# GLA mixing: the coarsest level's differences and exponentials made by ScalarE with biases per channel, and VectorE's wait for the masks put at the first masking

## The reference, cut to what matters

```python
def step(S, inp):
    q_c, k_c, v_c, b_c = inp
    o_inter = jnp.einsum('bhcd,bhde->bhce', q_c * jnp.exp(b_c), S)
    diff = b_c[:, :, :, None, :] - b_c[:, :, None, :, :]
    dmat = jnp.exp(jnp.where(mask, diff, -jnp.inf))
    scores = jnp.einsum('bhid,bhjd,bhijd->bhij', q_c, k_c, dmat)
    o_intra = jnp.einsum('bhij,bhje->bhie', scores, v_c)
    b_last = b_c[:, :, -1:, :]
    S = (S * jnp.exp(b_last[:, :, 0, :])[..., None]
         + jnp.einsum('bhcd,bhce->bhde', k_c * jnp.exp(b_last - b_c), v_c))
    return S, o_inter + o_intra
```

## Time and profile before

| | us |
|---|---|
| median of 3 executions | 3025.73 |
| lowest and highest | 3022.07, 3026.02 |
| the profiled execution, its own time | 3016.57 |
| its span in the profile | 3014.5 |
| PE, DVE, ACT, POOL busy over the span | 2873.7, 1460.5, 1157.9, 260.6 |
| the stage `gla_mix`, from the first to the last instruction of its own | about 210 to 328 |

### The profile page before, as it was taken

One profiled execution on the slowest core, in us unless ns is written; L12 is line 12 of the kernel. 1 busy time (PEld: TensorE's weight loads), 2 busy tenths in 40 slices (PEclk: granted clock), 3 DMA queues, 4 the chain that ended last, 5 costly groups with the idle time before them and its releaser, 6 DMA issues.

```text
span 3014.5 us, 57436 instructions
## 1 busy us (share of the span) xinstructions
PE 2873.7 (95%) x25392; PEld 2356.4 (78%) x25392; DVE 1460.5 (48%) x2048; ACT 1157.9 (38%) x1944; POOL 260.6 (9%) x306
## 2 busy tenths in 40 slices
PE   5987899799998999999999999999999999999997
PEld 5776677788885888888888888788888888888886
DVE  3669576455455644332443337674454534244323
ACT  4766664222224433322322245432244323233322
POOL 1000123544530000000000000000000000000000
PEclk8997899899998999999999999999999999999998
DMA  4320344211102232233222232223223232233222
GB/s 137 136 73 3 110 147 154 57 39 39 40 12 78 91 119 91 91 98 98 91 92 98 98 105 91 88 95 93 97 91 97 92 98 96 93 98 124 95 96 84
DMA packets 100439, 273.11 MB, mean 91 GB/s; under 512 B 9120, under 2 KB 36384, under 8 KB 100192
## 3 DMA queue, kind: packets, MB, share of 16 engines
q1 hardware_dynamic: 91408, 236.94, 24.3%
q0 software_dynamic: 8784, 32.51, 3.3%
HBM read 256.69 MB, written 12.58 MB: 89 GB/s over the span
## 4 chain that ended last, share of the span: by engine, by line
PE 66%; DVE 2%; ACT 1%; issue 0%; DVEq 0%; ACTq 0%
PE be_ps L3009 48%; PE be_ps L3062 16%; PE be_ps L3075 1%; DVE be_ring L2788 1%; PE be_ps L2733 1%; PE be_ps L2727 0%; PE be_ps L2412 0%; DVE be_raw_r L3257 0%; ACT be_whi L3112 0%; DVE be_total L2746 0%; DVE big L2760 0%; DVE big L2770 0%; DVE ext_r L2798 0%; DVE big_r L2798 0%; PE be_ps L2451 0%
## 5 line engine op out<-in xcount | busy, mean ns | idle before, releaser
L3257 DVE TENSOR_TENSOR be_raw_r<-be_raw,be_whi 128x1024 fp32r<-128x1024 f32 x361 | 442.4, 1225 | 974.2 <-ACT be_whi L3112 973.9
L3112 ACT CAST be_whi<-be_raw 128x1024 fp32r<-128x1024 f32 x361 | 378.9, 1050 | 891.6 <-DMA be_raw<-in_ffn_down 316.8
L3009 PE MATMUL be_ps<-ext_r,be_whi 128*128 128x512 f32 x2304 | 713.7, 391 | 6.8 <-DVE be_raw_r L3257 3.6
L3009 PE MATMUL be_ps<-big_r,be_whi 128*128 128x512 f32 x2048 | 642.1, 394 | 0.8 <-DVE be_raw_r L3257 0.5
L3009 PEld LDWEIGHTS be_ps<-ext_r,be_whi 128*128 128x128 f32 x2304 | 430.2, 188 | 102.6 <-DVE be_raw_r L3257 4.8
L3009 PEld LDWEIGHTS be_ps<-big_r,be_whi 128*128 128x128 f32 x2048 | 383.1, 188 | 95.7 <-DVE big_r L2796 1.0
L3009 PE MATMUL be_ps<-ext_r,be_raw_r 128*128 128x512 f32 x1152 | 448.4, 389 | 0.0
L3009 PE MATMUL be_ps<-big_r,be_raw_r 128*128 128x512 f32 x1024 | 408.0, 398 | 0.0
L3062 PE MATMUL be_ps<-ext_r,be_whi 128*128 128x512 f32 x1152 | 354.7, 389 | 0.0
L3009 PEld LDWEIGHTS be_ps<-ext_r,be_raw_r 128*128 128x128 f32 x1152 | 216.2, 188 | 45.2
L3062 PEld LDWEIGHTS be_ps<-ext_r,be_whi 128*128 128x128 f32 x1152 | 216.2, 188 | 45.2
(11 more groups left out here) (342 smaller groups left out, 3822.1 us busy)
## 6 DMA issues: line engine op xcount, KB each, us to landing
be_raw<-in_ffn_gate SPq DMA_DIRECT2D x88, 512.0 KB, 3.5
be_raw<-in_ffn_up SPq DMA_DIRECT2D x88, 512.0 KB, 3.5
be_raw<-in_ffn_down SPq DMA_DIRECT2D x88, 512.0 KB, 3.5
be_raw<-in_conv_in SPq DMA_DIRECT2D x48, 512.0 KB, 3.5
gp_ada<-in_ada POOLq DMA_DIRECT2D x24, 512.0 KB, 3.8
rp_ada<-in_ada POOLq DMA_DIRECT2D x24, 512.0 KB, 4.5
rwkv_prepared<-big SPq DMA_DIRECT2D x16, 512.0 KB, 3.2
be_raw<-in_w_out SPq DMA_DIRECT2D x16, 512.0 KB, 3.6
```

The lines of the kernel that those rows point to most:

```text
L3009: mm = pe.matmul(ps[:, bank], part[:, k * P:(k + 1) * P], xs(k), start=(k == order[0] and i == 0), stop=(k == order[-1] and i == 2))
L3112: act.copy(w.hi[:, n % 3], w.raw[:, n % 3]).then_inc(w.hi_ready, 1)
L3257: dve.tensor_tensor(w.lo(n), w.raw[:, n % 3], w.hi[:, n % 3].bitcast(F32), ALU.subtract).then_inc(w.lo_ready, 1)
```

## The change

ScalarE makes level 6 alone: two small copies write the two middle values, with either sign and divided by 16, to a new tile `middle`; after a wait for them, eight exponentials of 64 elements read `summed` directly, with the middle as bias per channel, and write the slot of the ring. VectorE's `diff6` is gone from all 8 turns. `copy_block(j)` waits for `diff5` and `exp6` of turn j-2 in place of `diff6`. The wait of VectorE for the masks moves from its first instructions to `masked(0)`.

```diff
-            dve_steps += ([f"diff{n + 2}"] if n + 2 < len(LEVELS) else []) + [f"qk{n}"]
+            dve_steps += ([f"diff{n + 2}"] if n + 2 < len(LEVELS) - 1 else []) + [f"qk{n}"]
...
+            def last_level_exp(j):
+
+                own, s, n = summed[:, j % 2], LEVELS[6], 6
+                between = bass.AP(tensor=own.tensor, offset=own.offset + s - 1, ap=[own.ap[0], [2 * BLK + 1, 2], [BLK, 2]])
+                for a in two:
+                    ins = act.activation(middle[:, a], between, ACT.Copy, scale=(-1 / 16, 1 / 16)[a])
+                ins.then_inc(*act_made("middle"))
+                level, before = ring_user(j, n)[1], ring_user(j, n)[0]
+                if before >= 0:
+                    act.wait_ge(*pe_made.by(f"score{level}", before))
+                act.wait_ge(*act_made.by("middle", j))
+                for a in two:
+                    for d in two:
+                        at_ = slice(0, s) if a != d else slice(s, BLK)
+                        for i in two:
+                            ins = act.activation(ring[:, slot(j, n), a, i, at_], own[:, d, i, at_], ACT.Exp,
+                                                 bias=middle[:, a, d, i:i + 1], scale=(1 / 16, -1 / 16)[a])
+                ins.then_inc(*act_made("exp6"))
...
                 if j >= 2:
-                    act.wait_ge(*dve_made.by("diff6", j - 2))
+                    act.wait_ge(*dve_made.by("diff5", j - 2))
+                    act.wait_ge(*act_made.by("exp6", j - 2))
...
-                level_exp(j, 6)
+                last_level_exp(j)
...
-            dve.wait_ge(loaded, 16)
...
                 dve.wait_ge(*pe_made.by("score4", j))
+                if j == 0:
+                    dve.wait_ge(loaded, 16)
...
-                    if n + 2 < len(LEVELS):
+                    if n + 2 < len(LEVELS) - 1:
                         level_diff(j, n + 2)
```

More of the change, by code:

```diff
@@ L837, in gla_mix @@
         end_sum = sb("end_sum", [P, 2, 2, 2])
+        middle = sb("middle", [P, 2, 2, 2])
         high = sb("high", [P, 2, 2, 2, BLK])
@@ L850, in gla_mix @@
         for n in levels:
-            dve_steps += ([f"diff{n + 2}"] if n + 2 < len(LEVELS) else []) + [f"qk{n}"]
+            dve_steps += ([f"diff{n + 2}"] if n + 2 < len(LEVELS) - 1 else []) + [f"qk{n}"]
             dve_steps += {6: ["state", "masked", "low"]}.get(n, [])
         act_steps = ["ends", "from_start", "to_end0", "to_end1", "exp0", "exp1", "v_tok0", "v_tok1", "k_tok", "exp2", "exp3",
-                     "exp4", "exp5", "exp6"]
+                     "exp4", "exp5", "middle", "exp6"]
         pe_steps = ["v_tok0", "diag", "v_tok1", "k_tok", "score0", "score1", "gain", "score2", "score3", "from_state",
```

## The result

The changed kernel took 3030.95 us (median of 20 executions, 3025.77 to 3043.99), the kernel before 3024.03 (20 executions, 3013.13 to 3034.66). The ratio is 1.0022, 95% interval 1.0012 to 1.0031: slower by 6.9 us in the medians, against a forecast of +5.1 and a median of 3030.8.

What follows compares the result with a forecast made beforehand. In `gla_mix`, turns 1 to 4 were bound by the chain TensorE, `take_outputs`, `exp4`, turns 5 to 7 by VectorE. 6.3 + 0.6 - 1.8 = +5.1 us, added to the median 3025.73, gave 3030.8 us, range 3024.5 to 3036.

Steps and rivals of the forecast that it cites:

- Part 1: VectorE loses `diff6`: 0.67 us a turn, worth that only where VectorE ends last, nothing by itself in turns 1 to 4.
- Part 2: ScalarE's `exp6` in ten pieces: large pieces 0.24 us apart, lasting 0.34; 2.42 us from ScalarE free until `qk6` can start.
- Part 3: VectorE's moved wait for the masks: the time goes into idle time before `qk2`, 0, bounds 0 to -1.57 us.
- Part 4: Moved guards of `copy_block` and level 6's ring slot: the work waited for is long done or done before `exp2`, 0.
- Turns 1 to 4: `qk6` waits for ScalarE's pieces and comes 1.58 us later in each turn, with nothing to absorb it: +6.3 us.
- Turn 0: `qk6` can start at 223.28 where it started at 222.69 before: +0.6 us.
- Turns 5 to 7: VectorE's own time bounds these turns and its output additions cover the pieces: -1.8 us.
- 0.61 of the 0.67 is kept: In turns 5 to 7 `qk6` can start at 305.25, 305.86 before, so most of the removed `diff6` is gained.
- the clock rival: TensorE's clock changes `from_block` and `add_low_scores`: slower +9.0 us, 3034.7, chance 0.15; faster -2.5, 3028.3, chance 0.06.
- The faster rival: VectorE bounds every turn and `exp6` stays hidden: -6.9 us, 3018.8, chance 0.04.
- The advice of the Trainium skill: Additions belong on VectorE, up to about 3 times faster per element in bf16; taken at its word +10.0 us, 3035.7, chance 0.02.

Runs made afterwards that it cites:

- e7_no_diff: The changed kernel with the level-6 pieces replaced by one plain exponential of 512 elements, `diff6` still left out; ratio to the kernel before 0.9990.
- e1_masks: The kernel before with only VectorE's wait for the masks moved to the first masking; ratio to the kernel before 1.0000.
- e2_level: The changed kernel with the masks' wait put back at the start, so the level-6 work alone; ratio to the kernel before 1.0019.
- e3_late: The changed kernel with the pieces in turns 5 to 7 only, `diff6` and one exponential in turns 0 to 4; ratio to the kernel before 0.9994.
- e6_sixteen: The changed kernel with sixteen pieces of 32 elements in place of eight of 64; ratio to the kernel before 1.0076, 4 executions.
- e4_middle: The changed kernel with the two middle copies moved up behind `v_tok0`; ratio to the kernel before 1.0013.
- e8_spread: The changed kernel with level 6 in its own tile, its pieces spread over ScalarE's idle places, `exp4` ahead of `take_outputs`; ratio to the kernel before 0.9986.
- e10_take: e8_spread with `take_outputs` ahead of `exp4` again; ratio to the kernel before 0.9985.
- e9_state: e8_spread with TensorE's `from_states` ahead of `score2` and `score3` in turns 1 to 4; ratio to the kernel before 0.9981.
- e5_exp4: The changed kernel with `exp4` ahead of `take_outputs` in turns 1 to 4; ratio to the kernel before 1.0021.

## Why the prediction was right

The mechanism was right: the pieces at the end of ScalarE's turn delay `qk6` in turns 0 to 4. That the median came within 0.2 us of the forecast's 3030.8 is luck. The median before that it started from, 3025.73 of three executions, was 1.7 above the 3024.03 of twenty, and the sum of 5.1 was 1.8 below the measured 6.9. The interval of the ratio, 1.0012 to 1.0031, is clear of no change, but lies on both sides of the 0.2% by which the prediction told "same" (0.60) from "slower" (0.36); between these two the runs don't decide.

*Part 1* held: `diff6` off VectorE is worth 0.65 in turn 0, nothing in turns 2 to 4 and about 0.7 where VectorE bounds the turn (e7_no_diff). *Part 2* held: distance 0.242 and duration 0.338 for the forecast 0.24 and 0.34, 2.45 for 2.42 to `qk6`. *Part 3* held: 0 (e1_masks). *Part 4*: no wait of `copy_block` or of the first copy for a guard appears in the trace.

*Turns 1 to 4* were forecast at +6.3 and came at +6.8, 1.7 a turn for 1.58. Between `qk4` and the state the new rows show 3.44 - 1.81 = 1.63; the rest, 0.05 to 0.1, lies on the way from the state to the next `qk4`. The comparisons at like durations on TensorE give 1.62 to 1.65 (e2_level) and 1.45 (e3_late), on both sides of the forecast. The idle time before `qk4` was named as 0.85 and was 1.35 to 1.65. It is 0.85 where only `diff6` is gone and TensorE's rows are unchanged (e7_no_diff), 0.68 and 0.64 in e2_level's turns with a short `from_block`, and 1.35 in those with 2.07: the excess goes with TensorE's clock, which the prediction had left as it was. *Turn 0* was forecast at +0.6 and came at +0.6, with 1.22 of idle time before `qk6` for the forecast 1.3.

*Turns 5 to 7* were mis-sized: -1.8 forecast, -0.6 measured. The step that failed is "0.61 of the 0.67 is kept" in each of the three. The pieces did stay hidden, but in turns 5 and 6 the state then waited 1.20 and 0.81 for TensorE's `from_state`, a stretch that my sum had not followed. Turn 7, without that wait, took 13.57 for 14.15 and kept 0.58. The rest of the stage, forecast at 0, cost 0.6: `add_low_scores` behind the last turn lasted 1.50 for 0.87. These two, 1.8 us together, both come from TensorE at its lower clock, though for turns 5 and 6 by another row than the one that the clock rival named; they account for most of the 2.4 between the sum and the trace's 7.5.

The clock rival had two ways to go, slower by `from_block` or faster by `add_low_scores`, and in the trace of the change both came at once in turns 1 to 4 and all but cancelled. `from_block` went from 1.57 to 2.07 in every one of these turns, and `add_low_scores` from 1.50 to 0.87, so that state to `qk4` took 11.82 before (262.33 - 250.51) and 11.87 after (267.81 - 255.94). That the two cancelled is luck too; the sum had no term for either. What the stage lost in these turns is the wait for the pieces; e6_sixteen and e4_middle move it up and down with their length, by 1.48 and 0.4 a turn at like durations on TensorE. The faster rival fell with e7_no_diff.

The advice of the Trainium skill ("ScalarE: Activation LUTs", Rules for kernel authors), to keep additions on VectorE, gave +10.0. Its sign was right for this change and its size too high by a third or more. e8_spread to e10_take show that the engine alone doesn't decide: with the same eight pieces on ScalarE the kernel is 0.14% to 0.19% faster than before.

## What to carry to other kernels

Before moving work to an idler engine, look at where in the turn that engine is idle, not how much: here ScalarE had 4 us free in a turn of 14, but none between `exp5` and the product that waits. A bias per channel splits one instruction into as many as there are biases, and short instructions cost their fixed part: give the pieces a buffer of their own and spread them over the idle stretches. And after taking work from the engine that seems to be the bound, ask which chain is late next; in the trace of e8_spread it was TensorE's `from_state`. When one trace is set against another, compare turns in which the clocked steps last equally long: here that turned 1.9 and 1.7 a turn into 1.48 and 1.62.

## What the runs showed of the hardware

TensorE's granted clock in this stage differed from trace to trace, and the length of the turn doesn't explain it. In turns of 13.63 (before, e1_masks, e7_no_diff) `add_low_scores` lasted 1.50 and `from_block` 1.55 to 1.65 nearly throughout; in the change's turns of 15.3 they lasted 0.87 and 2.07, four times in a row, with about the same mean clock (0.74 and 0.76 in the windows). But e3_late had 0.87 and 2.07 in nearly all of its turns of 13.57 to 14.07, and e2_level, with turns as long as the change's, 1.50 and 1.36 to 2.07. What sets the pattern stays open.

So a single profiled execution carries a scatter. Turns 5 to 7 have the same program in e8_spread, e9_state and e10_take and took 41.1, 43.4 and 41.3. The profiled execution of e5_exp4, with a stage 4 us shorter, had a span 7.2 us longer than the change's. Only the timed runs compare kernels; the trace compares steps.
